# Memory attention in a two-block model: values feature by token, weights divided before their transposes, gated outputs left untransposed

## The reference, cut to what matters

```
def memory_attention(q, mk, mv):
    s = einsum('bshd,bmhd->bhsm', q, mk) * (128 ** -0.5)
    p = softmax(s, axis=-1)
    return einsum('bhsm,bmhd->bshd', p, mv)

def mixer_layer(x, mem, ...):
    z = rmsnorm(x, g_norm) @ w_in
    dq, dk, dv, dg, lq, lk, lv, lg, mq, mg, mgate = split(z)
    y_a = (rmsnorm(diff_attention(dq, dk, dv)) * (1 - lam_init) * silu(dg)) @ w_br_diff
    y_b = (dilated attention of lq, lk, lv over 3 groups * silu(lg)) @ w_br_dil
    mem_n = rmsnorm(mem, g_mem);  mk, mv = split(mem_n @ w_mem_kv)
    o_m = memory_attention(mq, mk, mv)
    y_m = (o_m * silu(mg)) @ w_br_mem
    g = sigmoid(mgate)
    merged = g[0] * y_a + g[1] * y_b + g[2] * y_m
    return x + merged @ w_out
```

## Time and profile before

| what | value |
|---|---|
| runs shown | 2098.97, 2100.16, 2100.80 us, median 2100.16 us |
| span of the profiled execution, first to last instruction | 2098.7 us |
| mean granted TensorE clock | 0.957 |
| TensorE matmuls busy | 1828.7 us, 87% |
| TensorE weight loads busy | 1214.5 us, 58% |
| VectorE busy | 690.8 us, 33% |
| ScalarE busy | 380.8 us, 18% |
| GpSimd busy | 119.3 us, 6% |

### The profile page before, as it was taken

How to read it: one execution, slowest core, us unless ns; L and a number is a source line. 1 busy time by engine, 2 the same in 40 slices (tenths; PEclk the granted TensorE clock), 3 DMA queues, 4 the chain that set the end, 5 groups by cost and what they waited for, 6 DMA issues and landing times.

```text
span 2098.7 us, 34922 instructions
## 1 busy us (share of the span) xinstructions
PE 1828.7 (87%) x15046; PEld 1214.5 (58%) x15046; DVE 690.8 (33%) x1228; ACT 380.8 (18%) x881; POOL 119.3 (6%) x182
## 2 busy tenths in 40 slices
PE   8998676777688867776778999999999999999998
PEld 5656455545466655555454868646544768746543
DVE  5641110111043211111114043473652043573752
ACT  3511011001013110110012022222211022222221
POOL 1100000000000000000004003000230001100000
PEclk9999888988899998988999999999999999999999
DMA  8599999999999999999999834244456643443331
GB/s 331 181 377 419 420 421 420 420 420 420 420 397 407 420 420 420 420 420 420 420 399 271 223 137 154 95 161 159 133 192 169 161 160 130 132 160 121 130 121 60
DMA packets 156205, 590.69 MB, mean 281 GB/s; under 512 B 16528, under 2 KB 34320, under 8 KB 107024
## 3 DMA queue, kind: packets, MB, share of 16 engines
q1 hardware_dynamic: 147504, 569.53, 70.4%
q0 software_dynamic: 8544, 18.89, 3.7%
HBM read 579.98 MB, written 8.39 MB: 280 GB/s over the span
## 4 chain that ended last, share of the span: by engine, by line
PE 58%; DMA 24%; SPq 10%; DVE 5%; issue 2%; ACT 1%; DVEq 0%; ACTq 0%
DMA ring<-in_moe_w_dram 22%; PE ps L603 14%; PE ps L571 14%; PE ps L582 7%; SPq L1203 6%; PE ps L1479 4%; SPq L1212 2%; PE ps L577 2%; PE ps L1459 2%; SPq L1219 2%; PE ps L1514 2%; PE ps L487 1%; PE ps L1756 1%; PE ps L548 1%; DMA arena<-in_moe_w_dram 1%
## 5 line engine op out<-in xcount | busy, mean ns | idle before, releaser
L1479 PE MATMUL ps<-ring,xT 128*32 128x128 f32 x8192 | 304.7, 307 | 181.2 <-DMA ring<-in_moe_w_dram 174.6
L1479 PEld LDWEIGHTS ps<-ring,xT 128*32 128x32 f32 x8192 | 264.7, 121 | 244.6 <-DMA ring<-in_moe_w_dram 189.7
L571 PE MATMUL ps<-xT,ring 128*128 128x256 f32 x1408 | 310.1, 380 | 0.0
L571 PEld LDWEIGHTS ps<-xT,ring 128*128 128x128 f32 x1408 | 265.3, 190 | 39.8 <-issue 4.9
L2173 DVE TENSOR_TENSOR arena<-arena,ps 128x256 f32<-128x256 f32 x32 | 13.5, 421 | 556.4 <-ACT arena L1850 556.4
L1012 DVE TENSOR_TENSOR ring<-ring 128x2048 f32<-128x2048 f32 x56 | 128.4, 2292 | 154.9 <-PE ps L603 147.7
L1514 PE MATMUL ps<-arena 128*32 128x512 f32 x768 | 118.4, 600 | 33.8 <-DVE arena L2173 30.9
L1142 POOL DMA_DIRECT2D ring<-gap_bias x160 | 96.6, 671 | 807.8 <-DVEq L2346 459.9
L1459 PE MATMUL ps<-arena,x_tm 128*128 128x128 f32 x1024 | 137.8, 291 | 0.0
L1459 PEld LDWEIGHTS ps<-arena,x_tm 128*128 128x128 f32 x1024 | 129.3, 205 | 11.1 <-issue 11.1
L603 PE MATMUL ps<-ring,xT 128*128 128x512 f32 x288 | 130.1, 594 | 1.5 <-ACT arena L761 1.5
(11 more groups left out here) (299 smaller groups left out, 1935.0 us busy)
## 6 DMA issues: line engine op xcount, KB each, us to landing
ring<-in_moe_w_dram SPq DMA_DIRECT2D x287, 1024.0 KB, 26.0
arena<-in_moe_w_dram SPq DMA_DIRECT2D x89, 1024.0 KB, 26.7
ring<-in_w_in_dram SPq DMA_DIRECT2D x44, 2048.0 KB, 8.2
ring<-in_w_in_dram SPq DMA_DIRECT2D x16, 1024.0 KB, 12.2
ring<-in_w_br_diff_dram SPq DMA_DIRECT2D x4, 2048.0 KB, 10.6
ring<-in_w_out_dram SPq DMA_DIRECT2D x4, 2048.0 KB, 8.1
arena<-in_moe_w_dram SPq DMA_DIRECT2D x14, 512.0 KB, 15.0
ring<-in_w_mem_kv_dram SPq DMA_DIRECT2D x3, 2048.0 KB, 18.8
```

The source lines that it names most:

```text
L571: m = nc.tensor.matmul(bank[:, u * T:(u + 1) * T], w[:, k, f * P:(f + 1) * P], xT[:, k, :], start=(k == 0), stop=(k == KD - 1))
L1479: m = nc.tensor.matmul(ps[SL * q:SL * q + SL, g % 2, s * P:(s + 1) * P], xs[:, g % 2, k, s * SL:(s + 1) * SL], w[:, c0:c0 + 2 * P - 1:2], ...
```

## The change

Five edits: `values` of a memory head lets the weights' transposes move and the values stand, so that the output is feature by token; `weigh` divides a memory head's exponentials before they are transposed, and `turn` waits for that (`w_ready2`); chunk 19, the memory gate, is multiplied feature by token; `gated` writes the gated output of a memory head to `omT` directly with one operation, with the factor 0.5 in it; the transposes, copies and halvings of the gated outputs go, and the memory branch product waits for a new semaphore, `mem_ready2`. In a pair the weighting of a memory head now stands ahead of the weight differences, as that of a differential head does.

```diff
@@ -85,7 +85,7 @@
     plan += [(w[18], ("dil", 1), None), (w[19], ("dil", 2), None), (("br_diff", 0), ("dil", 3), None),
              (("br_diff", 1), None, None)]
     plan += [(w[22], ("mem", 0), "dil"), (w[23], ("mem", 1), None), (("br_dil", 0), ("mem", 2), None),
-             (w[24], ("mem", 3), None), (w[25], None, "mem"), (("br_mem", 0), None, None),
+             (w[24], ("mem", 3), None), (w[25], None, None), (("br_mem", 0), None, None),
              (("w_out", 0), None, None), (("w_out", 1), None, None)]
     return plan
 
@@ -107,7 +107,7 @@
 MAPS = dict(diff=2, mem=1)
 TURNS = dict(diff=1, dil=2, mem=1)
 JOB_SCALE = dict(diff=DQ ** -0.5, dil=HD ** -0.5, mem=HD ** -0.5)
-TILES = dict(diff=KD, dil=LH, mem=MH, merged=KD)
+TILES = dict(diff=KD, dil=LH, merged=KD)
 LAM0 = [0.8 - 0.6 * float(np.exp(-0.3 * l)) for l in range(DEPTH)]
 
 
@@ -312,8 +312,9 @@
         merged = dgt
         h_tm, x_sq, g_x = places(arena, 12288, AW - 3072, (TT, D), (2 * TT, CW), (D,))
         obT, omT, mergedT = places(arena, 8192, 8192 + 6144, (LH, T), (MH, T), (KD, T))
-        gate_of = dict(diff=dgt, dil=lgt, mem=mgt)
-        turned_of = dict(diff=oaT, dil=obT, mem=omT, merged=mergedT)
+        mgT = mgt.rearrange("p t n -> p (t n)").rearrange("p (h t) -> p h t", h=MH)
+        gate_of = dict(diff=dgt, dil=lgt)
+        turned_of = dict(diff=oaT, dil=obT, merged=mergedT)
         KH, COMBINED, TANHS = KD // 2, 2 + 4 * len(PAIRS), 20
         S1, S2, S3x = consts[:, P:P + KH * P], gap_rows[:, :], x_comb[:, 0:KH * P]
         S4_of = [arena[:, AW - 3 * P + k * P:AW - 2 * P + k * P] for k in range(3)] + [x_comb[:, KH * P:]]
@@ -389,6 +390,10 @@
         def products(l, n):
 
             return l * NHALF + n
+
+        def weighed(l, kind, h):
+
+            return l * (DH + MH) + (h if kind == "diff" else DH + h) + 1
 
         def turns(l, what):
 
@@ -522,10 +527,10 @@
                 i.then_inc(sem("s_full2"), 1)
 
             def turn(l, kind, h, J):
-                if kind == "diff":
-                    pe.wait_ge(sem("w_ready2"), l * DH + h + 1)
+                if kind == "dil":
+                    pe.wait_ge(sem("p_ready2"), l * NJOB + J + 1)
                 else:
-                    pe.wait_ge(sem("p_ready2"), l * NJOB + J + 1)
+                    pe.wait_ge(sem("w_ready2"), weighed(l, kind, h))
                 if kind == "dil":
                     turn_tiles([[S_dil[:, t, dil_cols(0, k)] for k in range(2) for t in range(TT)],
                                 [S_dil[:, t, dil_cols(m)] for m in (1, 2) for t in range(TT)]])
@@ -537,14 +542,15 @@
                     wait_taken(pe, l, chunk_of("w_in", 5))
                 pe.wait_ge(sem("turn_read"), turned[0])
                 pe.wait_ge(sem("o_taken2"), l * NJOB + J + 1)
+                if kind == "mem":
+                    for k in range(2):
+                        i = nc.tensor.matmul(ps[:, 7, 0:T], mv[:, k, h * HD:(h + 1) * HD],
+                                             PT3[:, 0, k * T:(k + 1) * T], start=(k == 0), stop=(k == 1))
+                    i.then_inc(sem("o_full2"), 1)
+                    return
                 for t in range(TT):
                     for k in range(2):
-                        if kind == "diff":
-                            v_ = dv[:, k, h * DV:(h + 1) * DV]
-                        elif kind == "dil":
-                            v_ = lv[:, k, h * HD:(h + 1) * HD]
-                        else:
-                            v_ = mv[:, k, h * HD:(h + 1) * HD]
+                        v_ = (dv if kind == "diff" else lv)[:, k, h * HD:(h + 1) * HD]
                         i = nc.tensor.matmul(ps[:, 7, t * P:(t + 1) * P],
                                              PT3[:, 0, k * T + t * P:k * T + (t + 1) * P], v_,
                                              start=(k == 0), stop=(k == 1 and kind != "dil"))
@@ -671,7 +677,7 @@
                     if job:
                         values(l, *job, job_n)
                         job_n += 1
-                pe.wait_ge(sem("turn_read"), turns(l, "mem") + TILES["mem"] // 2)
+                pe.wait_ge(sem("mem_ready2"), l + 1)
                 for half in range(3):
                     product(l, LASTS - 1, half)
                 turn_merged(l, 0)
@@ -688,7 +694,7 @@
                 assert turned[0] == 2 + (l + 1) * NTURN - (0 if l + 1 < DEPTH else 2) and job_n == NJOB
 
         def by_feature(name, c):
-            return name == "w_in" and (c < 4 or 8 <= c < 14 or c == 18)
+            return name == "w_in" and (c < 4 or 8 <= c < 14 or c in (18, 19))
 
         def squares(act, l, t):
             for c in range(2):
@@ -942,6 +948,11 @@
                     if kind != "diff":
                         v.wait_ge(sem("p_ready2"), l * NJOB + J + 1)
                         ch(nc.vector.reciprocal(rden3[:, 0:TT], den3[:, 0:TT]))
+                        if kind == "mem":
+                            for t in range(TT):
+                                part = S3[:, 0, t * T:(t + 1) * T]
+                                ch(nc.vector.tensor_scalar(part, part, rden3[:, t:t + 1], None, ALU.mult))
+                            v.sem_inc(sem("w_ready2"), 1)
                         return
                     v.wait_ge(sem("map_p"), l * DH + h + 1)
                     ch(nc.vector.reciprocal(rden3[:, 0:2], den3[:, 0:2]))
@@ -958,6 +969,13 @@
                 def gated(kind, h, J):
 
                     v.wait_ge(sem("o_full2"), l * NJOB + J + 2)
+                    if kind == "mem":
+                        ch(nc.vector.scalar_tensor_tensor(omT[:, h, :], ps[:, 7, 0:T], 0.5, mgT[:, h, :], ALU.mult,
+                                                          ALU.mult))
+                        v.sem_inc(sem("o_taken2"), 1)
+                        if h == MH - 1:
+                            v.sem_inc(sem("mem_ready2"), 1)
+                        return
                     g = gate_of[kind]
                     if kind == "diff":
                         v.wait_ge(sem("o_squared"), l * DH + h + 1)
@@ -977,7 +995,7 @@
                             part = dgt[:, t, :].rearrange("p (h d) -> p h d", h=DH)
                             ch(nc.vector.tensor_tensor(part, part, over(ssq16[:, :, t], 2, DV), ALU.mult))
                         v.sem_inc(sem("diff_ready2"), 1)
-                    elif kind != "diff" and h == LH - 1:
+                    elif kind == "dil" and h == LH - 1:
                         for t in range(TT):
                             ch(nc.vector.tensor_scalar(g[:, t, :], g[:, t, :], 0.5, None, ALU.mult))
                         v.sem_inc(sem(f"{kind}_ready2"), 1)
@@ -1039,11 +1057,11 @@
                     o11, o12, o21, o22 = pair_outputs(i)
                     if job0:
                         scale_max(*job0, job_n)
-                    if job0 and job0[0] == "diff":
+                    if job0 and job0[0] != "dil":
                         weigh(*job0, job_n)
                     combine_w(i, 0)
                     combine_w(i, 1)
-                    if job0 and job0[0] != "diff":
+                    if job0 and job0[0] == "dil":
                         weigh(*job0, job_n)
                     combine_w(i, 2)
                     wait_product_taken(v, l, unit_at(i, 0))
```

## The result

The changed kernel takes 2104.02 us in the median of 21 runs (2101.94 to 2106.88), the kernel before 2100.23 us (21 runs, 2098.82 to 2101.77): a ratio of 1.0017, 95% interval 1.0012 to 1.0023. It is 3.8 us or 0.18% slower, by 2.5 to 4.8 us (0.12% to 0.23%). The forecast was 2103.3 us. The profiled execution has a span of 2103.1 us.

The account below looks back on a forecast made before the run. TensorE was taken as the bound, nearly without holes around the memory heads. Stalls 0.45 + 0.96 + 1.03, minus 0.87 and 0.10, plus 0.08, gave +1.55 us a layer, +3.1 in two: 2103.3 us (+0.15%), 8-in-10 range 2099.6 to 2106.0.

Parts of the forecast that it names:

- Chunk 19: Memory gate multiplied feature-major: 32 instructions of 256 columns for 16 of 512 per half, +0.04 us a half, +0.08 a layer.
- The rule of the Trainium skill: Rival that weight loads aren't hidden: chunk 19 dearer by 12.2 us, values cheaper by 6.1, total 2109.3 us; chance 0.02.
- Values: Memory heads' value products: two of 256 columns replace four of 128, gaining 0.03 us a head, 0.1 us a layer.
- Head 0: First of chunks 22 and 23: transposes wait for the division, +0.45 us with weight load, bounds 0 and 1.1.
- Rival B: VectorE's order bounds pair 22/23, at the sixth unit and head 1's transposes: 0.6 to 1.5 us a layer; chance 0.18.
- Head 1: Second of chunks 22 and 23: transposes wait for VectorE's passed-on lateness, +0.96 us with weight load, bounds 0 and 2.1.
- Head 2: Beside the dilated branch product: already waiting transposes move to 1528.53, +1.03 us unhidden, bounds 0.7 and 1.35.
- Head 3: First of chunks 24 and 25: TensorE reaches its transposes late, so the division is hidden by 2.4 us; cost 0.
- Transposes of the gated outputs: Eight TensorE transposes a layer go and nothing is late in their place: gain 0.87 us a layer.
- The gating operation: On VectorE, two 128x128 operations of 0.74 us become one of 128x256, 0.46 us; off TensorE's path, worth nothing itself.
- rival A: Stalls of heads 0, 1 and 2 hidden: 2098.4 us with none, 2100.4 with head 2's alone; chance 0.17.

Follow-up runs that it names:

- head 0 undivided: Changed kernel without the first memory head's division, its reciprocal again behind two weight differences, its transposes waiting for the exponentials: 2102.27 us, ratio 1.0012.
- head 1 early: Changed kernel with the second memory head's weighting one addition sooner in VectorE's order, directly behind the fourth weight difference: 2103.30 us, ratio 1.0014.
- the two repeats: The changed kernel, unedited, run and profiled twice more: 2103.32 and 2101.42 us.
- head 2 late in the changed kernel: Changed kernel with the third memory head's transposes one product later, behind the second of the dilated branch's four products: 2098.84 us, ratio 0.9995.
- the two fastest reorderings: Changed kernel with head 2 late and head 1 early: 2098.06 us; also with dilated transposes first, head 0's weighting behind one difference, scaling wait mended: 2096.26 us.

## Why the prediction was right

By its own steps, first layer; times are counted from the first differential head's transposes at 1248.03 (before) and 1249.09 (after), 1.06 us apart, so that the first block's part is out.

- *Chunk 19*: +0.04 us a half forecast, 7.07 us for both halves measured, and 966.57 against 966.36 us alone. Right. The rule of the Trainium skill that the forecast weighed ("TensorE: Matmul & The Clock Gate", Back-to-back issue gap), by which weight load and matmul together set the spacing, would have made the narrow form dearer. This case's traces don't agree for float32: the half with twice the weight loads took 0.04 us more.
- *Values*: 1506.74 to 1507.60, 0.86 us for 0.89. Right.
- *Head 0*: 0.45 us forecast; its transposes are 0.50 us later, of which 0.10 us is chunk 19's, and unit 3 behind them 0.55 (1503.30 for 1501.69 below). Right, also that it passes to VectorE as a lateness of 2 us that TensorE's units don't feel: no unit waited for a difference. Rival B is out as it was stated, since the sixth unit didn't wait. Its other place, head 1's transposes, did feel VectorE running later than summed, by 0.4 us, less than the 0.6 us from which B was to decide.
- *Head 1*: 0.96 us forecast, with the weight load. Measured 1.42 to the unit behind it in the first layer (unit 6 at 1517.19 for 1514.19, cumulative 1.94 after 0.52) and 1.08 in the second. This is the one term that was mis-sized. About 0.1 us of it is in both layers: the sum has the third weight difference 0.04 us behind the second, and three of them in a row take 7.17 us in the second layer, which is 0.15 us between two. The other 0.35 us is in the first layer only, and its row is above: VectorE's third difference at 1506.71 has an idle time of 0.50 us behind the second one. The kernel before has the same pause behind the third difference (0.57 us of idle time at 1506.03, where the second layer shows 0.22); it was hidden there, and the change put it on the path. What causes it no run told.
- *Head 2*: +1.03 forecast, cumulative 1.91 (1525.78 for 1522.81) to 2.94: +1.03. Right.
- *Head 3*: no wait forecast, none shown. *Transposes of the gated outputs*: -0.87 forecast, cumulative 2.89 (1559.06 for 1555.11) to 2.01. Right. The gating operation took 0.42 us for my 0.46.

The rows of the kernel before that these differences are taken from, beside the earlier trace rows:

```profile
1501.69 3.60 PE L603 MATMUL ps<-ring,xT 128*128 128x512 f32 x8
...
1514.19 3.60 PE L603 MATMUL ps<-ring,xT 128*128 128x512 f32 x8
...
1522.81 3.60 PE L577 MATMUL ps<-ring,arena 128*128 128x512 f32 x8
```

The sum of the first layer is +2.01 us (1.55 forecast), of the second +1.31. In the second layer the kernel before had a wait of 0.32 us in an earlier pair, of differential heads, that the changed one didn't show. VectorE's rows there show the same pause: 0.57 us of idle time behind the third difference, and 0.22 us in the changed kernel. The two rows of the kernel before, then the changed kernel's:

```profile
1861.49 0.69 DVE L1018 TENSOR_TENSOR arena<-arena,ps 128x512 f32<-128x512 f32 x1 [0.57 <-DVE ring L1012]
1862.38 3.67 PE L603 MATMUL ps<-ring,gap_rows 128*128 128x512 f32 x8 [0.32 <-DVEq L1019]
```

```profile
1864.21 0.69 DVE L1036 TENSOR_TENSOR arena<-arena,ps 128x512 f32<-128x512 f32 x1 [0.22 <-DVE ring L1030]
```

With both taken out each layer is about 1.65. The second block thus gives +3.3 us for +3.1. That the total came so near is in part luck: the pause costs the changed kernel 0.35 us in the first layer and the kernel before 0.32 us in the second, and neither was in the forecast; had the second been hidden, the block would have grown by 3.6. The medians of all runs say +3.8; their interval holds both.

The experiments bear out the cause and not only the sum: without the division the block falls to 964.56 us, within 0.1 us of before minus the work removed (966.36 - 1.8 = 964.6); and rival A's floor, 2098.4 us, is what that kernel took (2098.30).

## What to carry to other kernels

Where one engine has no holes, price an edit by what it puts between that engine and its operands, not by the work it saves: here 1.8 us of transposes and columns were bought with 5.1 us of waits, for two products a head that hold VectorE for 0.74 us. Lateness in a strictly ordered queue is paid by whoever stands behind it, so look at the next two consumers, not at the edited one. The cheapest cure was the order on the waiting engine: moving one head's transposes a product later gained 2.6 us in the old kernel without touching the arithmetic.

## What the runs showed of the hardware that I had not expected

- *A short wait can cost nearly its length again in clock.* The profiles of this study hold 10 waits of 2.12 us in front of head 2. Behind two of them (one in each of the runs with head 0 undivided and with head 1 early) the granted clock fell from 1.00 to between 0.50 and 0.60 for about 3 us (from 2.4 GHz to the lower level of 1.2 GHz for most of them), which cost 1.7 and 1.6 us. Behind the other eight it stayed at 1.00, as it did behind the waits of 1.88 and 1.86 us that the kernel before has at its first differential heads. Behind 5.36 us of waiting it was at 0.50 in both layers. What decides whether it falls behind 2.12 us no run told. Both falls came on one chip, where four of the ten waits were; the four waits of the two repeats were on another and show none, so the chip isn't excluded. The spread of the runs without a profile decides nothing: 7.2 us with head 0 undivided and 3.0 with head 1 early, but 3.7 us over ten of the eleven runs with head 2 late in the changed kernel, which has no such wait, and 2.4 and 2.2 for the two fastest reorderings of it. The changed kernel's three profiles show no fall; whether some of its 21 runs had one, and whether that is in the 0.5 us between 3.3 and 3.8, stays open.
- *VectorE pauses for about 0.35 us at places that move with the program.* In the first layer's pair it is in all 13 profiles: behind the third weight difference in the kernel before and wherever head 0's two products don't stand ahead of it, and behind the second one where they do. In the second layer's memory pair it is absent, but the kernel before has it in a differential pair of that layer (1861.49 above); the changed kernel doesn't show it there, and without the division it stands one operation further on, at 1862.44 (0.58 us of idle time for 0.23). So it belongs to a place in the sequence of instructions rather than to an operation. In the ten profiles where it was looked for, one packet of 8 KB of the instruction queue q14 is on record 0.5 to 0.8 us behind the end of the first layer's pause (in the kernel before at 1506.6 for 1506.03, in the changed one at 1507.3 for 1506.71). That the two belong together is a guess; no run tested it.
